# Two transformer stacks on one core: each token half crosses the norm between two phases by itself

## The reference, cut to what matters

```python
# first stack, layer l of 2
x = x + 0.5 * swiglu(rms_norm(x, ffn1_norm[l]), ffn1_w13[l], ffn1_w2[l])
h = rms_norm(x, mix_norm[l])
...            # three attention branches from h @ w_in[l], gated, summed
x = x + jnp.sum(gates * proj, axis=2) @ w_out[l]
x = x + 0.5 * swiglu(rms_norm(x, ffn2_norm[l]), ffn2_w13[l], ffn2_w2[l])
# then rms_norm(x, final_norm); second stack, layer i of 4
x = x + 0.5 * rms_norm_2(swiglu_2(rms_norm_2(x, g[0]), ...), g[1])
hm = rms_norm_2(x, g[2])
m = (sliding_sink_attention, nsa_attention, moba_attention)[i % 3](hm, ...)
x = x + rms_norm_2(m, g[3])
x = x + 0.5 * rms_norm_2(swiglu_2(rms_norm_2(x, g[4]), ...), g[5])
```

## Time and profile before

| what | value |
|---|---|
| median of 3 runs | 3763.49 us (3762.18 to 3764.39) |
| the profiled execution | 3769.29 us |
| its span, first to last instruction | 3767.5 us |
| TensorE / VectorE / ScalarE / GpSimd busy | 91% / 58% / 48% / 2% |
| mean granted TensorE clock | 0.928 |
| loaded from HBM | 615.62 MB, 166 GB/s over the span |

### The profile page before, as it was taken

The page is one execution under the profiler, slowest core; times in us unless marked ns, Lnnn a source line. Parts: engine busy times, 40 slices in busy tenths (PEclk is TensorE's granted clock), DMA queues, the critical chain, the costliest instruction groups (busy, mean ns, idle before and its releaser), DMA issues.

```text
span 3767.5 us, 49512 instructions
## 1 busy us (share of the span) xinstructions
PE 3426.0 (91%) x18184; PEld 2934.5 (78%) x18184; DVE 2185.6 (58%) x2330; ACT 1800.3 (48%) x2261; POOL 92.5 (2%) x208
## 2 busy tenths in 40 slices
PE   7987899999778899997899998789999989998799
PEld 6876677878677788787787877678787978787687
DVE  5565465555655555556556565555655755556655
ACT  4455444444554444445444453344444544445444
POOL 0000000000000000000000000100000000000000
PEclk9998899999978999998999996679999999999899
DMA  6653344545333455454354543225454535454354
GB/s 237 216 190 112 111 167 180 184 179 189 145 107 118 156 189 184 172 185 154 132 187 169 192 164 134 67 101 196 172 189 173 182 146 181 173 195 168 106 196 167
DMA packets 105050, 618.45 MB, mean 164 GB/s; under 512 B 10816, under 2 KB 19008, under 8 KB 34656
## 3 DMA queue, kind: packets, MB, share of 16 engines
q1 hardware_dynamic: 84288, 562.07, 41.5%
q10 hardware_dynamic: 20640, 54.71, 4.4%
HBM read 615.62 MB, written 9.50 MB: 166 GB/s over the span
## 4 chain that ended last, share of the span: by engine, by line
PE 83%; DVE 7%; ACT 5%; issue 3%; DVEq 1%; DMA 1%; POOL 1%; ACTq 0%; POOLq 0%
PE ps L1529 32%; PE ps L1533 16%; PE ps L1593 6%; PE ps L1592 6%; PE ps L1594 6%; PE ps L1550 2%; PE ps L1551 2%; PE ps L1552 2%; PE ps L1568 2%; PE ps L1692 1%; DVE wlo L994 1%; PE ps L1681 1%; ACT v L645 1%; ACT whi L609 1%; PE ps L1706 1%
## 5 line engine op out<-in xcount | busy, mean ns | idle before, releaser
L1529 PE MATMUL ps<-xhl,whi 128*128 128x512 f32 x4944 | 1738.1, 401 | 34.8 <-DVEq L413 34.8
L994 DVE TENSOR_TENSOR wlo<-raw,whi 128x2048 fp32r<-128x2048 f32 x526 | 1204.2, 2292 | 806.4 <-ACT whi L609 806.3
L1533 PE MATMUL ps<-xhl,wlo 128*128 128x256 f32 x4944 | 1291.5, 282 | 0.0
L609 ACT CAST whi<-raw 128x2048 fp32r<-128x2048 f32 x526 | 999.8, 1904 | 251.9 <-PE ps L1594 128.0
L1529 PEld LDWEIGHTS ps<-xhl,whi 128*128 128x128 f32 x4944 | 907.1, 191 | 217.6 <-issue 41.8
L1533 PEld LDWEIGHTS ps<-xhl,wlo 128*128 128x128 f32 x4944 | 948.8, 192 | 55.6
L1593 PE MATMUL ps<-wlo,ht 128*128 128x512 f32 x1056 | 417.2, 395 | 0.0
L1592 PE MATMUL ps<-whi,ht 128*128 128x512 f32 x1056 | 417.1, 395 | 0.0
L1594 PE MATMUL ps<-whi,ht 128*128 128x512 f32 x1056 | 416.6, 395 | 0.0
L682 ACT COPY tg<-ps 128x512 f32<-128x512 f32 x132 | 77.5, 587 | 430.9 <-PE ps L1529 430.9
L1593 PEld LDWEIGHTS ps<-wlo,ht 128*128 128x128 f32 x1056 | 198.3, 188 | 48.1
(11 more groups left out here) (242 smaller groups left out, 3695.0 us busy)
## 6 DMA issues: line engine op xcount, KB each, us to landing
raw<-stream SPq DMA_DIRECT2D x528, 1024.0 KB, 4.8
bias<-rel_bias ACTq DMA_DIRECT2D x80, 256.0 KB, 2.7
gain<-gains ACTq DMA_DIRECT2D x19, 1024.0 KB, 4.7
bias<-fixed_bias ACTq DMA_DIRECT2D x40, 256.0 KB, 2.7
rel_bias<-rel_vectors SPq DMA_DIRECT2D x16, 512.0 KB
x<-x_tokens ACTq DMA_DIRECT2D x1, 1024.0 KB, 4.9
y_tokens<-x ACTq DMA_DIRECT2D x1, 1024.0 KB, 3.9
cst<-constants ACTq DMA_DIRECT2D x1, 670.0 KB, 6.7
```

The source lines that it names most:

```text
L609: nc.scalar.copy(whi[:, slot, :], raw[:, slot, :]).then_inc(sem["hi_ready"], 1)
L994: nc.vector.tensor_tensor(wlo[:, slot, :], raw[:, slot, :], whi[:, slot, :].bitcast(F32), ALU.subtract).then_inc(sem["lo_ready"], 1)
L1529: wide = lambda: pe.matmul(ps[:, bank, 0:2 * half], hi[:, k, col0:col0 + P], src[:, k0 + k, :], start=first and k == 0, stop=last and k == ...
L1533: e = pe.matmul(ps[:, bank, 0:half], lo[:, k, col0:col0 + P], src[:, k0 + k, 0:half], start=False, stop=False)
```

## The change

The operations on x are the same in number of columns; their pieces, their order and the place of several products change.

1. The norm work is cut into halves of 512 columns: squares, gains, additions and norms are two instructions where one was, and each half signals. GpSimd adds the two half sums of squares.
2. The order in `between` is by token half: half 0 goes through all its rounds before half 1's second part. The splits of the next phase's steps `step + 1` and `step + 2` stand inside the border now.
3. TensorE has no `between` of its own. The next phase begins with `arrive(ph, 0)` (the transposes of half 0), multiplies the first step or steps for half 0 as its high and low parts come, transposes half 1 (`arrive(ph, 1)`) in the midst of them, and does half 1.
4. The first pair of a feed-forward part is summed token by token (stationary x, 256 weight columns), h is made from banks 4 and 5 directly and transposed by four more transposes. The first pair's down step comes before the g step of pair 1.
5. The last pair uses `narrow_tile` and needs no additions. Its two down steps go by token half: both steps for half 0, `acc_half`, both for half 1. `wout` likewise; a weave ends with (3,0), (3,1), (2,3), (3,2), (3,3).
6. In the projections after a border the first step is a group of values, token-major, so the stream is put in another order (the first stack's 512 columns of values come as two groups of 256). gqa2 keeps its keys and values first and does both by token half.

```diff
-GQA_SLOTS = slots_of([part for j in range(2, 8) for part in quarters(j)],
-                     [2, 2] + [1] * 11 + [2, 2, 2, 2, 1, 0])
-MOBA_SLOTS = slots_of([part for j in range(3, 15) for part in quarters(j)],
-                      [3] * 12 + [2] * 6 + [0])
+GQA_SLOTS = slots_of([part for j in range(2, 8) for part in quarters(j)][:-1], [2, 2] + [1] * 13 + [2, 2, 1, 1])
+MOBA_SLOTS = slots_of([part for j in range(3, 15) for part in quarters(j)][:-1], [3] * 12 + [2] * 4 + [1] * 3)
...
-        project(f("q", 0, 2), f("k", 0, 2), t("v", 0, 512, 4, 2, 1))
+        project(t("v", 0, 256, 8, 1, 1), f("q", 0, 2), f("k", 0, 2), t("v", 256, 256, 8, 1, 1))
```

ScalarE, between: the end of it, with the order of the halves:

```diff
+                step = after_of(ph).step
+                first_statistics(0)
+                if per_token == 2:
+                    last_statistics(0)
+                    first_statistics(1)
+                if ph.gains == 0:
+                    split(0)
+                if per_token == 1:
+                    split(step + 1)
+                high_parts(0)
+                if per_token == 2:
+                    split(step + 1)
+                    last_statistics(1)
+                else:
+                    first_statistics(1)
+                split(step + 2)
+                high_parts(1)
```

VectorE, between:

```diff
+                if ph.after == "post":
+                    gained(0)
+                added(0)
+                if ph.final:
+                    final_norm(0)
+                normed(0)
+                if ph.after == "post":
+                    gained(1)
+                else:
+                    added(1)
+                if ph.gains == 0:
+                    split(0)
+                low_parts_of(0)
+                if ph.after == "post":
+                    added(1)
+                if ph.final:
+                    final_norm(1)
+                split(step + 1)
+                normed(1)
+                low_parts_of(1)
+                split(step + 2)
```

VectorE, ffn: the first pair and the last:

```diff
+                def first_pair(tt):
+                    dve.wait_ge(sem["silu_first"], base(ph, "silu_first") + tt + 1)
+                    nc.vector.tensor_tensor(h[:, tt, :], ps[:, 4 + tt, T:2 * T], silu[:, tt, :], ALU.mult)\
+                        .then_inc(sem["h_first"], 1)
+                first_pair(0)
                 split(ph.step + 3)
+                first_pair(1)
...
                 split(end - 1)
-                half_g(PAIRS - 1, 1)
+                dve.wait_ge(sem["step_used"], end - 2)
+                nc.vector.tensor_tensor(h[:, :, :], halves(ps[:, 2, :]), silu[:, :, :], ALU.mult)
```

TensorE: the products of a leading step c for one token half:

```diff
+            def lead_tokens(ph, dst, c, tt, between=None):
+                w = [part[:, c % RING, :].rearrange("p (k n) -> p k n", k=KD) for part in (whi, wlo)]
+                def products(token_part, weight_part, ks):
+                    for k in ks:
+                        at = token_part * T + tt * P
+                        e = pe.matmul(dst, xhl[:, k, at:at + P], w[weight_part][:, k, :],
...
+                high_made(c)
+                if c == ph.step:
+                    use(c)
+                    for half in range(2):
+                        high_arrived(ph, tt, half)
+                        ks = range(4 * half, 4 * half + 4)
+                        products(0, 0, ks)
+                        products(0, 1, ks)
+                    arrived(ph, tt)
+                    return products(1, 0, range(KD))
+                products(0, 0, range(KD))
+                if between is not None:
+                    between()
+                products(1, 0, range(KD))
+                use(c)
+                return products(0, 1, range(KD))
```

TensorE, ffn:

```diff
-                up(ph.step, 0)
-                up(ph.step + 1, 2)
-                body(1, ph.step + 2, first=True)
+                arrive(ph, 0)
+                for tt in range(TT):
+                    for part in range(2):
+                        e = lead_tokens(ph, ps[:, 4 + tt, part * T:(part + 1) * T], ph.step + part, tt,
+                                        (lambda: arrive(ph, 1)) if (tt, part) == (0, 1) else None)
+                        if tt == 1:
+                            e.then_inc(sem["step_used"], 1)
+                    if tt == 0:
+                        e.then_inc(sem["ag_made"], 1)
+                use(ph.step + 2)
+                w = step_parts(ph.step + 2, KD, 2 * P)
+                feature_tile(0, w, 0, xhl)
+                for tt in range(TT):
+                    pe.wait_ge(sem["h_first"], base(ph, "h_first") + tt + 1)
+                    for kk in range(2):
+                        e = pe.transpose(ps[:, 6, kk * T + tt * P:kk * T + (tt + 1) * P],
+                                         h[:, tt, kk * P:(kk + 1) * P], ident)
+                e.then_inc(sem["tposed"], 1)
+                feature_tile(1, w, P, xhl).then_inc(sem["step_used"], 1)
+                pe.wait_ge(sem["ht_first"], base(ph, "ht_first") + 1)
+                down(ph.step + 3, first=True)
+                up(ph.step + 4, 2)
...
+                for tt in range(TT):
+                    for i in range(2):
+                        c = end - 2 + i
+                        if tt == 0:
+                            pe.wait_ge(sem["ht_ready"], base(ph, "ht_ready") + last - 1 + i)
+                            use(c)
+                        w = step_parts(c, 2, D)
+                        for kk in range(2):
+                            e = rows_by(w, i, tt, kk, False, i == 1)
```

TensorE, weave:

```diff
-                for quarter in range(4 * ph.early):
+                arrive(ph, 0)
+                for tt in range(TT):
+                    if tt == 1:
+                        arrive(ph, 1)
+                    if ph.groups[0].dest == "v":
+                        e = lead_tokens(ph, ps[:, 4, tt * T:(tt + 1) * T], ph.step, tt)
+                    else:
+                        arrived(ph, tt)
+                        e = keys_and_values(tt)
+                e.then_inc(sem["step_used"], 1)
+                for quarter in range(4, 4 * ph.early):
                     product(quarter // 4, quarter % 4)
...
-                for quarter in range(4):
-                    out(n_g + 3, quarter)
+                for i, quarter in ((3, 0), (3, 1), (2, 3), (3, 2), (3, 3)):
+                    out(n_g + i, quarter)
```

TensorE, wout:

```diff
-                for i in range(4):
+                for i, tt in ((0, 0), (0, 1), (1, 0), (1, 1), (2, 0), (3, 0), (2, 1), (3, 1)):
```

449 lines of the change are left out of this document (267 added, 182 removed).

## The result

The changed kernel takes 3737.76 us (median of 4 runs, 3734.58 to 3738.82) against 3763.27 (4 runs, 3762.18 to 3764.39) before: a ratio of 0.9934, 95% interval 0.9919 to 0.9949. Taken again later beside other runs it gave 3733.21 and 0.9921 (0.9907 to 0.9934). So it is faster, by 25 to 31 us where 47 were forecast. The profiled execution has a span of 3737.0, 30.5 less than that of before.

What follows compares the result with a forecast made beforehand. TensorE was taken as the bound, with its idling at 18 borders to be shortened. Border gains of 47.6 us, minus 6 and 3.6 added work, plus 3 filler and 6 clock, gave 47 us: 3717 us, range 3684 to 3752.

Steps and rivals of the forecast that it cites:

- the sum: Post border, costed operation by operation: half 1 transposed from 15.3, lead done 18.8 after TensorE's end, taken as 19.0.
- The GpSimd pair: Border: half 1's mean square and power, let end 0.7 us after VectorE's weight split; if not held, 0.75 less per border.
- between no loss and a loss through all lead products I take the value that the nearest row has, 1.9: Post borders: 3.1 us of idleness stay behind a sparse stretch, so the clock loss stays at 1.9 us.
- 1.2 of 1.45 go: Plain borders, which norm once: shorter waits recover 1.2 of 1.45 us of clock loss each, 6 us in all.
- Rival A: All borders: the full clock is kept, the remaining 26 us of clock loss go too, 3690 us; chance 0.20.
- rival C: Borders: clock stays at 1.2 GHz from half 1's transposes through the lead, 115 us lost for today's 32, 3805; chance 0.09.
- 96 products of 128 columns at 0.11, 10.7 us: gqa2 leads: token-split keys eat 2.5 us of the gain, leaving 0.8 each, 1.6 together.
- into a projection only one step leads ... gain 2.7: Borders before projections: two plain and two post (nsa, moba) gain 2.7 us each, 10.8 in all.
- The four transposes of h: First pair of feed-forward parts: four added TensorE transposes cost 0.5 us in each of 12 parts, 6 us.
- The filler at a weave's end: Weave ends: a product part fills TensorE's 1.01 us wait for the heads' last low part, 3 us over three weaves.
- Rival B: All borders: GpSimd is not held by the weight split, 13 us more gained, 3704 us; chance 0.14.
- Rival D: Borders: no overlap, VectorE serves half 0 first and half 1 is late by as much; 3770 us, within 0.2%; chance 0.07.

Runs made afterwards that it cites:

- the run with the keys in the middle: Changed kernel, gqa2 leads as values of half 0, half 1's transposes, 256-column keys of both halves, values of half 1: 3717.92 us, ratio 0.9875.
- the late split: Changed kernel, VectorE finishing half 1's norm before it splits the second step's weights, in every border: 3715.31 us, ratio 0.9869.
- the combination: Changed kernel with keys mid-lead in gqa2, moba four groups ahead, projection sums before splits: 3704.55 us; with half 1's norm before the split too: 3685.85.

## Why the prediction was right in part

**The kind was right.** TensorE's idling at the borders bounded what the change could move, and it moved: a faster kernel, inside the range, 21 us above the forecast. The signs came true in the feed-forward part. Half 1's transposes came at 9.3 us where about 10 were forecast (9.7 by the sum), and the lead ended at 19.6 where 18 to 20 were. The GpSimd pair was held, and the norm behind it started at 8.5 us, 0.9 after the split's end (2686.39 against 2683.19 + 2.28). No wait for h stands before the last pair's down steps. One sign for wrong came too: the gqa2 leads took 21 us for their 96 products, where over 12 was the sign.

**The feed-forward borders: mechanism right, clock mis-sized.** By the sum a post border's lead should end 19.0 us after the last product without clock loss and 20.9 with it. It ended at 19.6, or 19.8 with the handover of 0.2 that the sum counts. The step that failed is "between no loss and a loss through all lead products I take the value that the nearest row has, 1.9". In the shown border the low stretch is 3.4 us, and such a stretch costs 1.5, as the run with the keys in the middle shows; without it the lead ends at 18.4 by the same count, so the sum was also 0.6 too long.

In the three borders behind a weave the loss was nothing. Their low stretch falls on half 0's products, and TensorE waits for half 1 after these in any case. One of them, with its last product at 1811.26:

```profile
1815.00:1818.40 3.40, 3.24 (x16) 3.21 (x16) 3.40 (x6) 3.38 (x6) 0.00 (x0) 0.50 0.03 5
1818.40:1822.00 3.60, 2.32 (x20) 2.12 (x19) 2.69 (x3) 2.21 (x3) 2.08 (x2) 1.00 0.06 14
```

Their leads end at 19.6, which is the 18.2 of a border without loss and the 1.4 us by which their overlap is shorter; the forecast was 22.3. So these three beat the sum by 7.6 us, and the other four by 3.9. Against that, the kernel before lost less in the seven than the border I took for all of them: its second steps end 22.6 to 25.3 us after the last product, 24.0 in the mean and not 24.46, which takes 2.9 back. That sums to 8.6 us, where these intervals beat the forecast by 8.3 (23.7 against 15.4).

In plain borders the term "1.2 of 1.45 go" was a little low: the three before a feed-forward part have no low stretch, and their lead ended at 15.7 us where 16.6 were forecast. Behind the final norm 4.9 us were gained where 1.5 were forecast; the record of the clock has 13.7 us low in this border before and 6.8 after, but no run took it apart.

Rival A, the full clock, was thus true in part: in the plain borders before a feed-forward part, by its cost in the three behind a weave, and with the late split in five post borders. In the shown border, with bursts 1 to 3 us apart, the clock was granted in full for the first 9 us. The Trainium skill, "TensorE: Matmul & The Clock Gate", section "HAM oscillation — how this bites in real kernels", has every burst after a wait begin at the lower rate; the waits of its example are 3 to 5 us, and the gaps in the changed kernel's borders are 1 to 3 us. By that rule, read without the length of the waits, C would have come. It did not: half 0's products of the shown border ran at 1.00 after a gap of 1.17 us. The trace agrees with it in the gqa2 leads and behind the weaves, where half 0's products ran at 0.50. That the clock then stays low through 10 us of busy TensorE, as it did in the gqa2 leads, is not in that section.

**gqa2: the term had the wrong sign.** The step was "96 products of 128 columns at 0.11, 10.7 us". The rate came from rows at the full clock. The products ran at 0.21, and the clock stayed low as long as the products had 128 columns, 27.3 us in all. In rival C I had priced this very outcome for gqa2 at about 10 us each. It was bound there to the same thing in all borders and so had a chance of 0.09, when it should have been judged for this lead alone. The order alone, keys or values first, was worth 8.0 us over the two weaves, and with the keys in the middle they gain 5 to 6.5 us each over the kernel before. So form and order are the cause.

**Projections: "into a projection only one step leads ... gain 2.7".** The lead did gain TensorE's time in the first stack, 3.9 us in layer 0 and 2.3 in layer 1, whose border has a low stretch of 3.4. The step failed since it stopped at TensorE. What follows a projection is an attention that waits for q, and q waits for ScalarE and VectorE to empty the groups. That wait was 5.14 us already in the kernel before, and the prediction named no row of it. With the values first, the groups of q and k come one step later against a chain that had no slack, and 3.0 us in either layer went into it. VectorE's order of split and sum is shown to set the length of this wait (8.14 to 4.34 us), but not that the mixer gains when it is gone. In moba the same displacement put 5.27 us in front of the first head, and taking the groups one slot sooner gave 3.6 us back. Of moba's loss of 7.1, which with the forecast gain makes an error of 10.8, half is not explained by a run. Counted from the traces, 3.8 of the 7.1 are the same products at a lower mean clock. nsa gained 4.1 where 2.7 were forecast, but with unchanged code it takes 283.7 to 287.5 from profile to profile.

**Small terms.** The four transposes of h take 0.35 us (2700.33 to 2700.68) where 0.5 was taken. The filler at a weave's end did what it was costed at: the three waits of 1.0 us are gone from the table. The other waits of the weaves' output steps are what they were: 1.7 us for ScalarE in moba in both kernels, and two for brw of 2.5 and 2.1 where the kernel before has two of 2.1.

**Rival B had the wrong size.** A border without the hold was priced 0.75 us shorter, 13 us in all. The edit that removes the hold took 18.7 us off in the combination. In the shown kind of border 0.4 of it is the hold and 1.5 the low stretch, which went with it in five of the borders; in plain ones 0.7 is the hold. **Rival D** is excluded by the products of half 0 at 2.6 to 6.6 us.

So the forecast was near for a reason that should not comfort: feed-forward parts 16 us better than forecast, mixers 32 us worse.

## What to carry to other kernels

When a wait at a border is shortened, follow the chain one consumer further than the engine that you freed: here the first stack's projections handed most of their gain to the engines that empty the groups, and one line of order on VectorE set 3.8 us of the wait. Cost products at both levels of the clock, and where a lead starts after a wait, try the 256-column products ahead of the 128-column ones. When an engine sits in a chain beside a long operation of another with two SBUF inputs, price the hold, and move the long operation behind it.

## What the runs showed of the hardware

With TensorE busy without a gap, the clock did not return during 48 products of 128 columns (10.3 us), while it returned 4.9 us into products of 256 columns. At the low level a product of either width started every 0.21 us (15 of 256 columns in 3.19 us, 49 of 128 in 10.30), and at the full level the 128-column ones came every 0.11 and the 256-column ones every 0.12, so half the columns bought no time at either level. A GpSimd TENSOR_SCALAR on 128x1 took 0.30 us alone and 1.51 beside VectorE's 128x2048 subtraction, and it ended with it. In the kernel before it was the power that was held, 1.48 us beside VectorE's addition, in the changed one the operation in front of it, so in both the hold fell on the one that started beside VectorE's operation with two inputs in SBUF. Where a gap of TensorE was shortened from 2.7 to 1.5 us, 3.4 us at the low clock became none in all eight borders seen; at 2.7 to 3.1 us the stretch was missing in one of 36, and 1.5 us went with it.
